# Two picks of 64 tokens in one gathered tile, and all picks added by TensorE

## The reference

```python
def peer_ffn(h, w_pq, subkeys, u, v):
    ...                      # scores; 8 heads, the best 16 of 16384 for each token and head
    def chunk(args):
        hc, ec, gc = args    # 128 tokens, their 8 x 16 expert numbers and gates
        u_sel = jnp.take(u, ec, axis=0)
        act = jax.nn.gelu(jnp.einsum('chkd,cd->chk', u_sel, hc), approximate=False) * gc
        v_sel = jnp.take(v, ec, axis=0)
        return jnp.einsum('chk,chkd->cd', act, v_sel)
```

## Time and profile before

| | us |
|---|---|
| median of 3 runs | 3601.86 |
| fastest, slowest run | 3600.21, 3602.8 |
| span of the profiled execution, first to last instruction | 3601.5 |

### The profile page before, as it was taken

One profiled execution on the slowest core, in us unless ns is written; L12 is line 12 of the kernel. 1 busy time (PEld: TensorE's weight loads), 2 busy tenths in 40 slices (PEclk: granted clock), 3 DMA queues, 4 the chain that ended last, 5 costly groups with the idle time before them and its releaser, 6 DMA issues.

```text
span 3601.5 us, 50492 instructions
## 1 busy us (share of the span) xinstructions
PE 3316.3 (92%) x18706; PEld 2633.5 (73%) x18706; DVE 2554.4 (71%) x4532; ACT 1537.0 (43%) x3089; POOL 770.5 (21%) x577
## 2 busy tenths in 40 slices
PE   7998889979898777799999999989999999999998
PEld 6886669855463222688777777767899988998898
DVE  6997143676777877687767777877867576768665
ACT  3222234245443333454444444545445443444443
POOL 1001236123435666122122122222200000000000
PEclk9999999999999999899899999999999999999999
DMA  3332224569999999699888899879956844453455
GB/s 123 94 95 75 75 83 141 182 272 397 407 415 421 417 411 418 261 377 389 324 321 312 305 372 385 317 296 341 374 176 188 267 141 131 133 184 106 140 184 156
DMA packets 184174, 918.82 MB, mean 255 GB/s; under 512 B 21536, under 2 KB 26912, under 8 KB 118128
## 3 DMA queue, kind: packets, MB, share of 16 engines
q0 software_dynamic: 73728, 536.90, 37.4%
q1 hardware_dynamic: 99248, 358.66, 29.9%
q10 hardware_dynamic: 10960, 20.12, 1.8%
HBM read 907.80 MB, written 7.80 MB: 254 GB/s over the span
## 4 chain that ended last, share of the span: by engine, by line
PE 72%; DVE 9%; DMA 7%; issue 5%; ACT 4%; POOL 2%; ACTq 0%; DVEq 0%; POOLq 0%
PE psum L715 54%; PE psum L1068 11%; DMA buffer_float<-in_peer_uv,buffer_uint 7%; DVE buffer_bfloat L2578 2%; POOL buffer_float L3259 2%; PE psum L1289 1%; ACT slabs_rounded L1452 1%; PE psum L723 1%; DVE buffer_float32r L2185 1%; PE psum L1274 1%; DVE norm_recip_root L2193 1%; DVE slabs_remainder L2279 1%; PE psum L1286 1%; PE psum L1372 1%; PE psum L1336 1%
## 5 line engine op out<-in xcount | busy, mean ns | idle before, releaser
L715 PE MATMUL psum<-buffer_float32r,slabs_rounded 128*128 128x256 f32 (+2 forms) x9568 | 2005.4, 309 | 70.3 <-POOL slabs_remainder L3244 30.1
L715 PEld LDWEIGHTS psum<-buffer_float32r,slabs_rounded 128*128 128x128 f32 x9568 | 1556.1, 192 | 217.3 <-issue 113.5
L715 PE MATMUL psum<-buffer_float32r,slabs_remainder 128*128 128x256 f32 (+2 forms) x4784 | 1439.8, 301 | 0.0
L2279 DVE TENSOR_TENSOR slabs_remainder<-raw_slabs,slabs_rounded 128x1024 fp32r<-128x1024 f32 x601 | 732.8, 1223 | 452.2 <-ACT slabs_rounded L1452 434.1
L1452 ACT ACTIVATE slabs_rounded<-raw_slabs 128x1024 fp32r<-128x1024 f32 x662 | 695.7, 1055 | 698.5 <-PE psum L715 620.7
L1068 PE MATMUL psum<-buffer_float,buffer_float 128*128 128x512 f32 x1712 | 825.2, 612 | 137.8 <-ACT buffer_float L1753 124.5
L715 PEld LDWEIGHTS psum<-buffer_float32r,slabs_remainder 128*128 128x128 f32 x4784 | 918.1, 192 | 29.8
L3259 POOL DMA_INDIRECT buffer_float<-in_peer_uv,buffer_uint x512 | 623.2, 1217 | 1330.8 <-PE psum L1068 753.6
L2578 DVE CUSTOM_DVE_ANT_0 buffer_bfloat<-buffer_float,buffer_float 128x1024 bf16<-128x1024 f32 x512 | 625.3, 1221 | 169.5 <-DMA buffer_float<-in_peer_uv,buffer_uint 160.8
L1068 PEld LDWEIGHTS psum<-buffer_float,buffer_float 128*128 128x128 f32 x1712 | 304.3, 193 | 519.6 <-issue 509.7
L1742 ACT ACTIVATE buffer_float<-buffer_float 128x1 f32<-128x1 f32 x512 | 100.3, 196 | 368.5 <-DVE buffer_float L2578 366.6
(11 more groups left out here) (213 smaller groups left out, 2039.0 us busy)
## 6 DMA issues: line engine op xcount, KB each, us to landing
raw_slabs<-in_slabs SPq DMA_DIRECT2D x682, 512.0 KB
buffer_float<-in_peer_uv,buffer_uint POOLq DMA_INDIRECT x512
buffer_float<-kept ACTq DMA_DIRECT2D x4, 874.5 KB, 6.0
xT<-in_xT ACTq DMA_DIRECT2D x4, 512.0 KB, 5.7
buffer_float<-in_consts ACTq DMA_DIRECT2D x8, 256.0 KB
kept<-buffer_float ACTq DMA_DIRECT2D x4, 512.0 KB
buffer_float<-kept ACTq DMA_DIRECT2D x2, 875.0 KB, 6.7
kept<-buffer_float ACTq DMA_DIRECT2D x4, 272.0 KB
```

What stands on the lines that cost most here:

```text
L715: m = pe.matmul(out, a, b, start=start and j == 0, stop=stop and j == 2)
L2279: dve.tensor_tensor(slab_l[:, r, :], raw[:, r, :], slab_h[:, j, :].bitcast(F32), ALU.subtract)\
```

## The change

- A gathered tile no longer holds one pick of 128 tokens but two picks of 64: partitions 0 to 63 take the even pick of tokens 0 to 63 of a group, partitions 64 to 127 the odd pick of the same tokens. There are 8 groups of 64 tokens with 64 gathers each, still 512 gathers of 128 rows. Numbers and gates are written in this order by half tiles (4 copies where 1 was, 4 products where 1 was).
- For the dot each token's row must lie on both partition halves. For groups 0 and 1 ScalarE copies it so from PSUM (`twin_rows`). For the others the rows are stored to memory and loaded twice, 64 partitions each (`load_rows`), into two buffers in turn.
- `diag` is 128 x 64: two 64 x 64 identities on top of each other, scaled. The product gives 64 output rows, the sum of the tile's two picks.
- Two gathered tiles are added together (`weigh_two`): the first to PSUM partitions 0 to 63 from columns 0 to 63 of the array, the second to partitions 64 to 127 from columns 64 to 127. In each bank two matmuls, 4 in all, where two picks had 4. TensorE waits for both gathers and both diagonals.
- `turn_rows` multiplies `out_rows` with the two stacked identities, which adds the two halves and turns them: 8 matmuls into one bank, for each of 8 groups.
- VectorE adds no picks; `by_dve`, `add_row` and `add_sums` are gone. ScalarE takes all sums.
- `TURN` has 4 entries, the woven borders after 64, 128, 192 and 256 gathers: slabs 63, 118, 171 and 230.

```diff
-TURN = (turn_after(PICKS), turn_after(WOVEN))
+BOUNDS = [GROUP * (j + 1) for j in range(WOVEN // GROUP)]
+TURN = [turn_after(n) for n in BOUNDS]
 def added_by(t, behind=3):
     n = woven_by(t - behind)
-    return PICKS if n > PICKS and t < TURN[0] + 3 else n
-def by_dve(n):
-    return n >= PURE and n % PICKS % 3 == 2
+    for bound, turn in zip(BOUNDS, TURN):
+        if n > bound and t < turn + 3:
+            return bound
+    return n - n % 2
...
-        diag = part(SLOTS, P)
+        diag = part(SLOTS, H64)
...
-            def weigh(n):
+            def weigh_two(n):
+                i = n % GROUP
+                if i == 0:
                     sums_at[:] = [acc.take(), acc.take()]
-                pe.wait_ge(uv_landed[slot], 16 * turn + 16)
-                pe.wait_ge(diag_done, DIAGONALS[n + 1])
+                for j in range(2):
+                    pe.wait_ge(uv_landed[(n + j) % SLOTS], 16 * ((n + j) // SLOTS) + 16)
+                pe.wait_ge(diag_done, n + 2)
                 for q in range(2):
                     b = sums_at[q][0]
...
-                    m = pe.matmul(psum[:, b, :], diag[:, slot, :], uv_rows[slot][:, D + q * 512:D + (q + 1) * 512],
-                                  start=p == 0, stop=p == PICKS - 1)
+                    for j in range(2):
+                        slot = (n + j) % SLOTS
+                        m = pe.matmul(psum[j * H64:(j + 1) * H64, b, :], diag[:, slot, :],
+                                      uv_rows[slot][:, D + q * 512:D + (q + 1) * 512], start=i == 0,
+                                      stop=i == GROUP - 2)
+                        if j and i == GROUP - 2:
+                            m.then_inc(bank_full[b], 1)
+                        elif q:
+                            m.then_inc(uv_used[slot], 1)
...
+                for k in range(KT):
+                    m = pe.matmul(psum[:, bn[0], k * H64:(k + 1) * H64], out_rows[:, k * P:(k + 1) * P], stacked,
+                                  start=True, stop=True)
...
+            def load_rows(g):
+                t, s = g // 2 - 1, g % 2
+                for c in range(2):
+                    act.dma_start(hrow[g][c * H64:(c + 1) * H64, :], rows_d[t, s * H64:(s + 1) * H64, :])\
+                        .then_inc(rows_here[s], 16)
...
-                if by_dve(n):
-                    return
                 if turn:
                     act.wait_ge(uv_used[slot], turn)
                 act.wait_ge(coef_done, n + 1)
-                act.activation(diag[:, slot, :], ident[:, :], ACT.Copy, scale=coefs[:, slot:slot + 1])\
+                act.activation(diag[:, slot, :], stacked, ACT.Copy, scale=coefs[:, slot:slot + 1])\
                     .then_inc(diag_done, 1)
+                g = n // GROUP + 2
+                if n % GROUP == GROUP - 1 and g < GROUPS and g not in (QT, QT + 1):
+                    ...
+                    load_rows(g)
...
-                step(dve.tensor_copy(eidx[:, tt, h0 * TOPK:h1 * TOPK], pk.fin_af[:, some].rearrange("p a b -> p (a b)")))
+                two = pk.fin_af[:, some].rearrange("p h (i c) -> p c (h i)", c=2)
+                for s in range(2):
+                    for c in range(2):
+                        step(dve.tensor_copy(eidx[c * H64:(c + 1) * H64, 2 * tt + s, h0 * TOPK // 2:h1 * TOPK // 2],
+                                             two[s * H64:(s + 1) * H64, c]))
```

More of the change, by code:

```diff
@@ L620, in build @@
         picked = sem("peer_picked")
+        rows_made = sem("stream_rows_made")
+        rows_kept = sem("stream_rows_kept")
+        rows_here = [sem(f"stream_rows_here_{p}") for p in range(2)]
         uv_landed = [sem(f"uv_landed_{j}") for j in range(SLOTS)]
@@ L1103, in weigh_to @@
                 while woven[0] < n:
[L1104 to L1106 removed]
+                    weigh_two(PURE + woven[0])
+                    woven[0] += 2
             def fill(behind=2):
@@ L1770, in _ @@
             turned = None
-            for tt in range(2):
-                sums = [acc.take(), acc.take()]
-                for p in range(PICKS):
-                    n = tt * PICKS + p
-                    coefficient(n)
-                    if n - STEP_LAG in STEPS:
-                        next(steps)
-                    if n in GATE_PICK:
-                        gate_exps(GATE_PICK[n])
-                take_sums(tt, sums, turned)
-                turned = [at.take(), at.take()]
+            for n in range(PURE):
+                if n % GROUP == 0:
+                    sums = [acc.take(), acc.take()]
+                coefficient(n)
+                if n - STEP_LAG in STEPS:
+                    next(steps)
+                if n in GATE_PICK:
+                    gate_exps(GATE_PICK[n])
+                if n > GROUP and n % GROUP == TURN_AT + STEP_LAG:
+                    turned = at.take()
+                if n == LATE_ROWS:
+                    act.wait_ge(rows_kept, 16 * (QT - 1))
+                    load_rows(QT)
+                    load_rows(QT + 1)
+                if n % GROUP == GROUP - 1:
+                    take_sums(n // GROUP, sums, turned)
+            turned = at.take()
             assert next(steps, None) is None
-            acc.take(), acc.take()
+            sums = [acc.take(), acc.take()]
             place, woven = [0], [0]
@@ L2068, in stream_squares @@
             def stream_squares(h, dst):
-                for bn in turned:
-                    emptied(bn)
+                emptied(turned)
                 for k in range(KT):
@@ L2547, in make_gates @@
                 sync()
-                step(dve.tensor_tensor(gates[:, tt, :].rearrange("p (h k) -> p h k", h=PEER_HEADS),
-                                       pk.fin_e, pk.fin_r.unsqueeze(2).to_broadcast([P, PEER_HEADS, TOPK]), ALU.mult))
+                two = pk.fin_e.rearrange("p h (i c) -> p c h i", c=2)
+                by = pk.fin_r.unsqueeze(2).to_broadcast([P, PEER_HEADS, TOPK // 2])
+                for s in range(2):
+                    mine = slice(s * H64, (s + 1) * H64)
+                    for c in range(2):
+                        out = gates[c * H64:(c + 1) * H64, 2 * tt + s, :].rearrange("p (h k) -> p h k", h=PEER_HEADS)
+                        step(dve.tensor_tensor(out, two[mine, c], by[mine], ALU.mult))
                 sync()
@@ L2716, in _ @@
                     make_gates(GATE_PICK[n - 7])
[L2717 to L2718 removed]
+                if n > GROUP and n % GROUP == TURN_AT + STEP_LAG:
+                    turned = at.take()
+            turned = at.take()
             assert next(choosing, None) is None and next(steps, None) is None
[L2720 to L2750 removed]
+            add_rows(QT - 1, turned)
+            acc.take(), acc.take()
+            place, woven, turned_at = [0], [0], [None]
             def point():
```

203 lines of the change are left out of this document (87 added, 116 removed).

## The result

| | before | after |
|---|---|---|
| median | 3601.03 us (4 runs beside it) | 3677.88 us (3674.02 to 3681.6, 4 runs) |
| ratio, 95% interval | | 1.0218 [1.0203, 1.0232] |
| profiled span | 3601.5 us | 3672.1 us |

The change makes the kernel 2.2% slower. The forecast was 3584 us, in a range of 3560 to 3640: sign and range are both wrong.

The account below looks back on a forecast made before the run. DMA was taken to bound the pure stage, TensorE the woven one. Woven -53 +5 +8 +8 +1 +4 = -27, pure +3 +3, before it +3: -18 us on 3601.5, so 3584, range 3560 to 3640.

Parts of the forecast that it names:

- Part 7, the ring: Pure stage: first slot held one pick longer, its new gather has 7.1 us to land, second slot unchanged; +3 us.
- The ring rival: Pure stage: overlap works, but the held slot starves DMA; +40 us, about 3625; chance 0.13.
- The clock: Pure stage: 1.2 GHz listed as a sign of being wrong, releasing pairs 1.7 us later; no term of its own.
- Part 5, rows through memory: Stores and loads of the stream's rows: +7.7 us pure, +1 woven; -5 back from faster picks; pure net +3.
- Part 1, the overlap: Woven picks on TensorE: column halves overlap fully, 1.72 + 0.18 us a pair, 243 us instead of 296; -53 us.
- half-overlap rival: Picks on TensorE: records taken in program order, only 3 borders shared, 2.33 us a pair; +29 us, 3630; chance 0.10.
- none: Picks on TensorE: no overlap of column halves, 3.62 us a pair; about +195 us, 3795; chance 0.14.
- Parts 2 and 3, turning and borders: Woven stage: sums turned four times instead of twice, +5 us; three inner borders instead of one, +8 us.
- Part 8, the woven dots: Woven VectorE: -12 us for additions it loses, +16 for dots waiting on later gathers; +4 us.
- Part 4: Two woven stretches where DMA is saturated too: the pick gain can't be taken there, -53 becomes -45; +8 us.
- Part 6: Before the first pick: VectorE writes each head's numbers by 4 copies instead of 1, with more gate products; +3 us.
- the 3558 us: Whole kernel: the time if nothing but parts 5 and 6 stood against the 53 us gain.

Follow-up runs that it names:

- f_warm3: The changed kernel with three filling matmuls on constants behind each pair of groups 2 and 3, to keep TensorE at work: ratio 1.0168, pure stage 742.2 us.
- e_before_hold: The kernel before, with TensorE adding pure-stage picks two by two when both are ready: ratio 1.0116, 3640.27 us, pure stage 732.9 us.
- a_single: The changed kernel, but the pure stage adds each pick alone as soon as it is ready, on its own column half: ratio 1.0057, 3619.49 us.
- h_noload: a_single without the stores and loads of the stream's rows (output not the reference's): ratio 0.9996, pure stage 683.9 us.
- b_serial: The changed kernel, with both picks of nearly all pure-stage pairs on the same column half: ratio 1.0237, pure stage 766.4 us.
- v_mixed_up: The changed kernel with single 128-token pure-stage picks, woven rows doubled on chip, and pairs added a slab sooner in the mixer's first part: ratio 0.9927, 3574.93 us.
- g_noborder: The changed kernel without the woven borders at 64 and 192 gathers (output not the reference's): ratio 1.016, woven stage 1119.5 us.
- c_warm: The changed kernel with two filling matmuls on constants behind each pair of groups 2 and 3: ratio 1.0163, pure stage 746.5 us.

## Why the prediction was wrong, point by point

**Part 7, the ring: this step failed.** It said that the first gather of a pair has 7.1 us to land, that the second has what it had, and took +3. The 7.1 us was about right at the full clock: 7.6 us from dot to issue in f_warm3, against 5.2 before, leave 6 x 2.49 - 7.6 = 7.3. What failed is the step that followed, that the 9.66 us are queue and shrink as far as needed. They shrank to 8.4 us for the first gather, with 3.13 gathers on the way in the mean in place of 3.90, and DMA moved 364 GB/s instead of 415. The second did not have what it had: 7.98 us from dot to issue, where it was 5.20, and its gather stood behind its partner's. Adding two by two in the old layout alone costs 39 to 46 us (e_before_hold), and giving it up in the new one brings 46 to 58 back, the clock's part included (a_single). The ring rival named this, at 50 us less what is given back, and had a chance of 0.13. Its 8.16 us was the right size, but not as a limit: the gather before it in the same chain took 5.57.

```profile
2073.58 5.57 DMA buffer_float<-in_peer_uv,buffer_uint
```

**The clock** was named among the things that would prove the forecast wrong, with the right effect (the release 1.7 us later; 9.24 against 7.6), but had no chance and no term. In the traces TensorE was busy 0.77 of the late pure stage at 1.00 before and is busy 0.53 at 0.72 after. It costs 13 to 16 us of 35 to 38 in groups 2 and 3, and 20 us of the whole by the medians (f_warm3), both with the filling matmuls in the way. The hold costs more in the new layout than in the old, 58 us against 39 by the medians, and the 20 us of the clock are as much as that; that the clock is all of it is not shown.

**Part 5, rows through memory:** +7.7 by bytes, 20.0 measured; the -5 that a faster pick should give back isn't seen in the pure stage as a whole (h_noload's 683.9 against 686.6 is 3 at most). A mis-sized term, 12 us.

**Part 1, the overlap: right,** and the price for changing shape right in kind. Its 0.18 us is 0.32: 8.06 us for a pair and two slabs, less two slabs of 3.01 (4.73 less 1.72), is 2.04 us a pair, or 1.72 + 0.32. Over 128 pairs, with the turnings, the woven TensorE work shrank by 30 us (the stage less its idle time) instead of 48. The Trainium skill's sentence that matmuls start and end strictly in program order (TensorE: Matmul & The Clock Gate, Part 3, The mechanism) agrees with this trace: the record of the second half starts and ends 0.01 to 0.04 us behind that of the first. It orders starts and ends and forbids no overlap; the prediction read its half-overlap rival into it, by taking the two records of a matmul as a block that the next has to wait for. Here they alternate between the halves, and eight take 1.94 us where b_serial's eight on one half take 3.62. Half overlap (0.10) and none (0.14) are refuted.

**Parts 2 and 3, turning and borders:** +13 for two more, 12 to 17 measured.

**Part 8, the woven dots:** the waits were feared in the right place (the mixer's short steps), but priced at +16 over the whole stage. In the mixer's first part one line that gives slots back sooner brings about 15 us; elsewhere no run shows that they cost anything. What VectorE's 110 us less of work are worth no run isolates.

**Part 4** can't be told apart from these. **Part 6** was right: +3 forecast, 3.3 measured, with L2573's copies at 168 ns each. A slip in the working: the 3558 us, for nothing against the gain but parts 5 and 6, should be about 3555.

Where the time went: pure stage 46.2 (hold and clock) + 20.0 (rows) - 2.7 (what is left) = 63.5. Woven stage -30.4 (TensorE work) + 26.9 (its idle time, 49.3 to 76.2 us) = -3.5. Both sums must come out as measured, since their terms are differences of the same profiles; they divide the time and prove nothing. Of the 27 us of idle time v_mixed_up took 11 away in quarter 2, and g_noborder 10 in all.

## What to carry to other kernels

That a transfer in a ring is "mostly queue" is an assumption until the ring has been seen with fewer on the way. No single row of the trace settles it: with the gather of 5.57 us in the trace before, (7.6 + 5.57) / 6 = 2.2 us would have passed against the 2.49 us per gather, and with 8.16 it is 2.6. What prices a common release is a run of the old kernel with nothing but one more wait, as e_before_hold, made before anything else is built. A change that helps where TensorE is the bound should be made there alone: in the stage where DMA is the bound it had nothing to win, and there it lost 63.5 us. And the price of a wait is read from the stage it stands in: of 88 us of waiting dots, some 15 were won back, in one quarter.

## What the runs showed of the hardware

- A gather of 128 rows of 8 KB takes longer the more are on the way: from issue to dot 8.1 us in median behind two others and 9.0 to 9.7 behind three (before, e_before_hold, after); the shortest took 5.4 to 5.6. With 3.13 on the way in the mean instead of 3.90, DMA moved 364 GB/s instead of 415.
- Two gathers issued 1.24 us apart (after, median) were dotted 2.48 us apart, as were gathers issued 2.48 us apart before.
- Two float32 matmuls on column halves begin within 0.01 us and cost about the time of one: 1.94 us for eight records of 512 columns, 3.62 for eight on one half, 3.50 for eight on two halves at 1.2 GHz.
- Going from 128 columns to halves and back costs TensorE some 0.3 us a pair between slabs (8.06 us for a pair and two slabs).
- The clock fell behind a late pair even with filling matmuls in between: in c_warm a pair took 1.94 us at 1355.53 and the next, behind 2.48 us without work, 3.46.
- 3.1 MB in eight loads and two stores, with the waits for them, took 20 us from a stage full of gathers, 2.6 times their share by bytes (a_single 703.9, h_noload 683.9).
